# Two more buffers for gathered expert rows, placed where the streamed U tiles lie, once the last of these has been used

## The reference

```python
def gmlp_mix(xn, w_in, g_v, w_s, b_s, w_out): ...      # layer 0 token mixer
def banded_attention(q, k, v, ...): ...                # layer 1 token mixer, window of 128

def peer_ffn(xn, w_q, sub_keys, exp_u, exp_v):         # both layers, every token on its own
    ...
        q = (xb @ w_q).reshape(blk, PEER_HEADS, 2, D_HALF)
        sc = jnp.einsum('thpd,hpnd->thpn', q, sub_keys).astype(jnp.float32)
        top_s, top_i = lax.top_k(sc, PEER_TOPK)
        cand_s = top_s[:, :, 0, :, None] + top_s[:, :, 1, None, :]
        cand_i = top_i[:, :, 0, :, None] * N_KEYS + top_i[:, :, 1, None, :]
        best_s, sel = lax.top_k(cand_s.reshape(blk, PEER_HEADS, PEER_TOPK * PEER_TOPK), PEER_TOPK)
        idx = jnp.take_along_axis(cand_i.reshape(...), sel, axis=-1)
        gate = jax.nn.softmax(best_s, axis=-1)
        act = jax.nn.gelu(jnp.einsum('thkd,td->thk', exp_u[idx], xb))
        w = (gate * act.astype(jnp.float32)).astype(xb.dtype)
        return jnp.einsum('thk,thkd->td', w, exp_v[idx])

def trunk(x, ck, cv):                                  # for 512 prompt tokens and 64 sample tokens
    for l in range(DEPTH):                             # DEPTH = 2
        ...                                            # token mixer, h = h + y
        hf = rms_norm(h, norm_ffn[l]).reshape(B * L, D_MODEL)
        h = h + peer_ffn(hf, peer_w_q[l], peer_sub_keys[l], peer_u[l], peer_v[l]).reshape(B, L, D_MODEL)
        ...
```

## Time and profile before

| | |
|---|---|
| median of three runs | 3457.68 us (3442.8 to 3468.78) |
| the profiled execution | 3455.63 us, its span 3453.5 us |
| TensorE busy | 87% of the span |
| VectorE busy | 73% |
| ScalarE, GpSimd busy | 23%, 29% |
| DMA traffic | 1043.13 MB, mean 302 GB/s |
| gathers | 640 indirect DMAs, 671.13 MB |

### The profile page before, as it was taken

How to read it: one execution, slowest core, us unless ns; L and a number is a source line. 1 busy time by engine, 2 the same in 40 slices (tenths; PEclk the granted TensorE clock), 3 DMA queues, 4 the chain that set the end, 5 groups by cost and what they waited for, 6 DMA issues and landing times.

```text
span 3453.5 us, 46623 instructions
## 1 busy us (share of the span) xinstructions
PE 3012.7 (87%) x17310; PEld 2621.0 (76%) x17310; DVE 2514.5 (73%) x5433; ACT 808.9 (23%) x2386; POOL 1009.3 (29%) x840
## 2 busy tenths in 40 slices
PE   6899979999999997666688989799999999997565
PEld 6787868988888886555566857689888888885454
DVE  3377787777777778777633786988777777787777
ACT  3332212211111111111244452222111111111112
POOL 4431022222222223333254410122222222222332
PEclk9899989999999998777786978899999999998887
DMA  4225678999999999999521346679999999999996
GB/s 154 87 94 205 250 274 328 357 394 393 380 393 397 382 397 345 351 368 365 217 97 31 109 159 229 238 281 371 381 387 395 399 392 397 390 376 357 364 363 237
DMA packets 159975, 1043.13 MB, mean 302 GB/s; under 512 B 18480, under 2 KB 23920, under 8 KB 44096
## 3 DMA queue, kind: packets, MB, share of 16 engines
q0 software_dynamic: 92160, 671.13, 49.9%
q1 hardware_dynamic: 63648, 357.59, 27.5%
q10 hardware_dynamic: 4000, 12.36, 1.0%
HBM read 1033.28 MB, written 7.86 MB: 301 GB/s over the span
## 4 chain that ended last, share of the span: by engine, by line
DMA 35%; PE 32%; DVE 20%; issue 9%; ACT 1%; POOL 1%; SPq 0%; DVEq 0%; ACTq 0%; POOLq 0%
DMA gat<-uvg,idxg 35%; PE bank L695 9%; DVE acc L1568 9%; PE bank L499 7%; DVE gat L1560 3%; PE bank L486 3%; PE bank L488 3%; PE bank L487 3%; DVE oneA L1535 2%; PE bank L682 2%; DVE B L1541 2%; PE bank L584 1%; PE bank L516 1%; DVE E L1530 1%; PE bank L838 1%
## 5 line engine op out<-in xcount | busy, mean ns | idle before, releaser
L1245 POOL DMA_INDIRECT gat<-uvg,idxg x640 | 735.7, 1150 | 2074.3 <-DVE acc L1568 2005.9
L708 PE MATMUL bank<-a,V 128*128 128x256 f32 x4096 | 997.1, 406 | 216.8 <-DVE a L1552 216.6
L1560 DVE CUSTOM_DVE_ANT_0 gat<-gat,xrow 128x1024 f32<-128x1024 f32 x640 | 781.5, 1221 | 519.1 <-DMA gat<-uvg,idxg 514.8
L708 PEld LDWEIGHTS bank<-a,V 128*128 128x128 f32 x4096 | 837.3, 206 | 359.4 <-issue 230.1
L695 PE MATMUL bank<-xd,U 128*128 128x256 f32 x4096 | 926.1, 385 | 0.5 <-DMA U<-uvd 0.5
L695 PEld LDWEIGHTS bank<-xd,U 128*128 128x128 f32 x4096 | 780.4, 193 | 104.3 <-DMA U<-uvd 1.3
L1568 DVE SCALAR_TENSOR_TENSOR acc<-gat,wgt,acc 128x1024 f32<-128x1024 f32 x640 | 818.8, 1279 | 39.7 <-ACT wgt L1054 39.5
L1052 ACT ACTIVATE act<-dot 128x1 f32<-128x1 f32 x640 | 128.9, 201 | 1508.9 <-DVE dot L1560 1508.7
L682 PEld LDWEIGHTS bank<-B,oneA 128*128 128x128 f16 x4096 | 282.6, 150 | 34.0 <-DVE oneA L1535 19.4
L682 PE MATMUL bank<-B,oneA 128*128 128x32 f16 x4096 | 285.5, 246 | 19.7 <-DVE oneA L1535 17.6
L499 PE MATMUL bank<-xd,raw 128*128 128x256 f32 x1088 | 248.7, 386 | 7.5 <-DVE xd L1332 7.1
(11 more groups left out here) (192 smaller groups left out, 2278.3 us busy)
## 6 DMA issues: line engine op xcount, KB each, us to landing
U<-uvd SPq DMA_DIRECT2D x128, 1024.0 KB
V<-uvd SPq DMA_DIRECT2D x128, 1024.0 KB, 8.7
raw<-lin SPq DMA_DIRECT2D x152, 512.0 KB
gat<-uvg,idxg POOLq DMA_INDIRECT x640
hsp<-h ACTq DMA_DIRECT2D x2, 2304.0 KB, 13.9
hx<-hsp SPq DMA_DIRECT2D x2, 2304.0 KB, 13.9
sk_g<-skT ACTq DMA_DIRECT2D x2, 1024.0 KB, 4.9
sk_d<-skT ACTq DMA_DIRECT2D x2, 1024.0 KB, 8.1
```

The source lines that it names most:

```text
L708: mm = pe.matmul(bank[b][:, TD * (d % 2):TD * (d % 2) + TD], V[:, s, o:o + P], a[:, s, TD * k:TD * k + TD], start=(first and k == 0 and d ...
L1245: pool.indirect_dma_start(gat[:, s % SLOTS, :], None, uvg[l], bass.IndirectOffsetOnAxis(idxg[:, s:s + 1], 0)).then_inc(g_in[s % SLOTS], 16)
L1560: dve.tensor_tensor_reduce(gat[:, s % SLOTS, 0:D], gat[:, s % SLOTS, 0:D], xrow[:, min(s // P, 2), :], 1.0, 0.0, ALU.mult, ALU.add, dot[:, ...
```

## The change

The gathers get six buffers instead of four, for part of each layer. `slots(l)` builds a table, for every step the buffer and the step that used it last. Steps below `first` = step0(l, 40) + 2 (224 in layer 0, 226 in layer 1) use the four buffers of `gat`, steps from `first` to 311 use six (numbers 4 and 5 are `U[:, 0]` and `U[:, 1]`), and steps 312 to 319 use the four again. Each time the buffer that has rested longest is taken. Where only four are in use, the gather of step s waits for axpy(s - 4) as before; from the third of the extended steps to step 313 it waits for axpy(s - 6). The first gather into either U buffer waits for the last scores that read this buffer. The loads of "kvd" wait, beside the last scores, for the axpy of step 311. No instruction is added, removed or moved on any engine; buffers, semaphores and the values waited for change.

```diff
@@ -290,7 +290,7 @@
         a_done, sums_done, hsum_done = sem("a_done"), sem("sums_done"), sem("hsum_done")
         xr_done = sem("xr_done")
         u_in, v_in = [sem(f"u_in{s}") for s in range(2)], [sem(f"v_in{s}") for s in range(2)]
-        g_in = [sem(f"g_in{s}") for s in range(SLOTS)]
+        g_in = [sem(f"g_in{s}") for s in range(SLOTS + 2)]
         gsel_done = sem("gsel_done")
         acc_zero, dot_done, act_done, wgt_done, ax_done = (
             sem(n) for n in ("acc_zero", "dot_done", "act_done", "wgt_done", "ax_done"))
@@ -308,6 +308,29 @@
         def step0(l, i):
 
             return EARLY[l] + i * (NSTEP - EARLY[l]) // NPAIR
+
+        def slots(l):
+
+            first, last = step0(l, NPAIR - RING) + 2, NSTEP - 8
+            used, table = [-1] * (SLOTS + 2), []
+            for s in range(NSTEP):
+                k = min(range(SLOTS + 2 if first <= s < last else SLOTS), key=lambda j: (used[j], -j))
+                table.append((k, used[k]))
+                used[k] = s
+            return table
+
+        SLOT = [slots(l) for l in range(2)]
+        FILLS = [[sum(k == j for k, _ in SLOT[l]) for j in range(SLOTS + 2)] for l in range(2)]
+
+        def row(l, s):
+
+            k = SLOT[l][s][0]
+            return gat[:, k, :] if k < SLOTS else U[:, k - SLOTS, :]
+
+        def landed(l, s):
+
+            k = SLOT[l][s][0]
+            return g_in[k], 16 * (l * FILLS[0][k] + sum(j == k for j, _ in SLOT[l][:s + 1]))
 
         def scored(i):
 
@@ -371,6 +394,7 @@
             elif name == "kvd":
                 for b in range(2):
                     eng.wait_ge(full[b], BASE["peer0"][b] + NPAIR // 2)
+                eng.wait_ge(ax_done, NSTEP - 8)
             else:
                 eng.wait_ge(*tile_done(last, k))
 
@@ -1240,10 +1264,14 @@
 
             def gather(l, s):
 
-                if s >= SLOTS:
-                    pool.wait_ge(ax_done, NSTEP * l + s - SLOTS + 1)
-                pool.indirect_dma_start(gat[:, s % SLOTS, :], None, uvg[l],
-                                        bass.IndirectOffsetOnAxis(idxg[:, s:s + 1], 0)).then_inc(g_in[s % SLOTS], 16)
+                k, last = SLOT[l][s]
+                if last >= 0:
+                    pool.wait_ge(ax_done, NSTEP * l + last + 1)
+                elif k >= SLOTS:
+                    b = k - SLOTS
+                    pool.wait_ge(full[b], BASE[f"peer{l}"][b] + NPAIR // 2)
+                pool.indirect_dma_start(row(l, s), None, uvg[l],
+                                        bass.IndirectOffsetOnAxis(idxg[:, s:s + 1], 0)).then_inc(g_in[k], 16)
 
             def experts(l):
 
@@ -1556,8 +1584,9 @@
 
             def dot_x(l, s):
 
-                dve.wait_ge(g_in[s % SLOTS], 16 * (NSTEP // SLOTS * l + s // SLOTS + 1))
-                dve.tensor_tensor_reduce(gat[:, s % SLOTS, 0:D], gat[:, s % SLOTS, 0:D], xrow[:, min(s // P, 2), :],
+                u = row(l, s)[:, 0:D]
+                dve.wait_ge(*landed(l, s))
+                dve.tensor_tensor_reduce(u, u, xrow[:, min(s // P, 2), :],
                                          1.0, 0.0, ALU.mult, ALU.add, dot[:, s % 8:s % 8 + 1]).then_inc(dot_done, 1)
 
             def axpy(l, s):
@@ -1565,7 +1594,7 @@
                 n = min(s // P, 2)
                 dve.wait_ge(wgt_done, NSTEP * l + s + 1)
                 dve.wait_ge(ax_done, NSTEP * l + s)
-                dve.scalar_tensor_tensor(out=acc[:, n, :], in0=gat[:, s % SLOTS, D:RD], scalar=wgt[:, s % 8:s % 8 + 1],
+                dve.scalar_tensor_tensor(out=acc[:, n, :], in0=row(l, s)[:, D:RD], scalar=wgt[:, s % 8:s % 8 + 1],
                                          in1=acc[:, n, :], op0=ALU.mult, op1=ALU.add).then_inc(ax_done, 1)
 
             def gathered(l, s):
```

## The result

The changed kernel takes 3360.81 us (median of four runs, 3353.97 to 3364.46) against 3456.56 us before (median of four, 3442.8 to 3468.78). The ratio is 0.9725, with a 95% interval of 0.9704 to 0.9746: about 95 us less. The prediction was 3429.0 us with a range that ended at 3405, so the direction was right and the size was not: the gain is more than three times the forecast.

What follows compares the result with a forecast made beforehand. The prediction took a four-buffer ring of gather, dot and axpy to bound both layers' tails. From 3455.6 us it took 16.4 and 16.2 us, added 6 for the wait on scores: 3429.0 us, range 3405 to 3455.

Steps and rivals of the forecast that it cites:

- What bounds the kernel now: Late in each layer no engine is full; the cycle gather, dot, axpy, gather sets 3.7 us a step with four buffers.
- The tails: End of the U tiles' use to each expert stage's end: 1332 to 1687 us and 3070 to 3421 us, together 706 us.
- The pace of the ring, (L + 2.7) / 3: In the tails, a turn carries three steps; a fetch of L = 8.42 us gives 3.7 us a step, six buffers 2.2.
- L itself is mostly queueing, because the DMA engines are 93% busy: In the tails, the fetch time L, 8.42 us on the chain, was said to be mostly waiting in DMA queues.
- The speed in the tails is 358 / 0.93 = 385 GB/s ... so I keep its own speed: Tails: only the busy share rises, 0.93 to 0.975, at 385 and 383 GB/s; gains 16.4 us (layer 0), 16.2 (layer 1).
- the first rival: DMA engines also get faster per byte: both tails at 394 GB/s, 32 and 33 us gained, 3396 us; chance 0.17.
- the second rival: Memory limits the tails at 356 to 358 GB/s, pace stays 3.7 us: 3455.6 or 3462 us; chance 0.15.
- The first use of the U buffers: Switch to six buffers: free in layer 0; in layer 1 step 226's gather waits about 12 us for scores, costing 6 us.
- The third rival: Layer 1, gather of step 226: waiting on the scores costs VectorE's 10.3 us, 3466 us if nothing is gained; chance 0.08.
- The loads of "kvd": End of layer 0: four loads delayed until about 1660 us take 5.5 us and stay hidden.
- V tiles behind a deeper queue: In the tails a V tile lands in 7.9 us with some 28 us available; even doubled it stays hidden.
- VectorE "is not the limit over the tail": VectorE needs 2.8 us a step (256.6 us for 93 steps), not the limit over the tail, though near in its first part.

Runs made afterwards that it cites:

- without V: V tiles of pairs 42 to 63 cut to 16 columns: 3382.6 us from the kernel before (four buffers), 3282.61 us from the changed kernel (six).

## Why the prediction was right and wrong

**What bounds the kernel now**: right. The tails were bound by the ring gather, dot, axpy, gather, and nothing else. Taking the extra fetches away restores the old time, and the dose from three to six buffers follows.

**The pace of the ring, (L + 2.7) / 3**: right in form. It gives the pace with three buffers too: the fetch there takes 6.5 and 6.7 us on average in the two tails, (6.6 + 2.7) / 2 = 4.65, and the trace has 4.5 to 4.8 us. For the kernel before I had taken 8.42 us, the longer of the two fetches of the earlier trace rows, without a reason; that it came near the average, about 8 us by the packet records, was luck. The fetches on the chain grew, to 12.1 to 17.7 us, where 14.8 was forecast. Wrong was the sentence "L itself is mostly queueing, because the DMA engines are 93% busy": without V, at 320 GB/s, it still takes 7.3 us, and no fetch of the two tails with three buffers takes less than 5.3. The step from the old pace to the forecast did not use this sentence.

**"The speed in the tails is 358 / 0.93 = 385 GB/s ... so I keep its own speed"**: this is the step that failed, and with it both large terms of the sum. A busy share of 0.93 was read as 7% of room. The room was 15%: 358 of 421 GB/s. The share counts slow packets as busy, and there are slow packets as soon as the demand leaves pauses. So neither the share nor rate over share is a measure of what is left. Layer 0: forecast 16.4 us, measured 45.4. Layer 1, before its loss: forecast 16.2, measured 40.7 with the loss in it. The share that I forecast as 0.975 was 0.99 over the tails; the speed at full share, forecast as 385 and 383 GB/s, was 421 / 1.01 = 417 in their middle.

The row that I should have asked for was in the old trace. The DMA view of the kernel before, 1332 to 1432 us, in slices of 2.5 us, share and rate:

```profile
DMA  9999988999979997898999989999897999999997
GB/s 403 416 429 406 377 334 226 344 334 383 347 279 347 419 426 279 370 403 236 364 331 351 334 298 357 419 416 331 328 426 203 357 328 410 347 315 334 416 367 305
```

and of the changed kernel, 3100 to 3300 us, in slices of 5 us, with its traffic and queue:

```profile
GB/s 421 418 419 423 432 430 414 421 419 424 418 423 423 423 415 421 421 421 421 424 419 424 421 421 419 424 419 421 419 423 416 423 419 424 426 421 419 421 419 419
DMA packets 11380, 84.27 MB, mean 421 GB/s; under 512 B 1258, under 2 KB 1258, under 8 KB 1258
...
q0 software_dynamic: 8986, 65.41, 78.6%
```

Before, the rate swings between 203 and 429 while the share hardly moves; its peaks, 416 to 429, are what the engines can do. After, it stands at 421 all the time. With 421 GB/s in the sum the forecast would have been 127.1 MB / 421 = 302 us and 125.09 / 421 = 297 us, 53 and 54 us gained, less 6: 3355 us. The rate over the whole tails was 410 and 408, for the two ends of the stretch.

**"Then both tails run at 394 GB/s" (the first rival)**: this rival named the right thing, faster packets, and still stopped too low, at 3396 us. The stage at 2950 to 3050 us is not limited by the DMA engines. TensorE is busy for all of it, and its pace asks for two tiles and four gathers every 16 us, 6.3 MB / 16 us = 393 GB/s. I took a demand for a limit. The changed kernel runs this stage at the same 390 to 398 GB/s.

**The memory as limit (the second rival)**: refuted, also by the forecast's own row of 394, and now by 421. The Trainium skill, "DMA: Bandwidth & Descriptors", section "Specifications", has about 358 GB/s per core from HBM; here one core, the only one at work, read 421 GB/s for 200 us.

**The first use of the U buffers**: right in the main. Layer 0: GpSimd waited 3.26 us for the scores where I had forecast no wait, but VectorE did not wait. Layer 1: a wait of GpSimd of about 12 us forecast, 10.43 measured; of VectorE 10.3 forecast, 8.14 measured; 6 us of DMA time forecast, 5.6 measured. What it costs, by the tails with and without the stop, is 3 to 8 us of layer 1; the term was 6. **The third rival** had the right price for the wait and the wrong weight: the tails gave eight times as much.

**The loads of "kvd"** and **V tiles behind a deeper queue**: right that they are hidden. The loads go at 1608.53 us and are first read at 1654.65 us. VectorE's waits in the tail show no TensorE sums among them. In the run with five buffers a V tile took 9.0 us to land, against 6.8 us in the same layer before. The cost of four buffers over the last eight steps, which I had put into the share of 0.975, is 9 us in layer 0.

**VectorE "is not the limit over the tail"**: right with V (162 of 200 us busy in the middle of layer 1's tail); without V it is close to it, at 173 of 180 us, with the DMA engines full beside it.

## What to carry to other kernels

When a ring of buffers holds a transfer-bound stage, work out what the ring allows per turn and take as the next limit the peak rate that short slices of the trace reach, not the mean rate divided by the busy share. Check whether the fullest stage of the kernel is full by its limit or by its demand: bytes per turn over the time of a turn tells. Try the number of buffers as a dose; here one more buffer gave the same time as two, and the other could have gone to something else; the second was worth 5 us in layer 0, and in layer 1 it brought a stop at the switch that cost as much as it gave. Where whole times scatter by more than the effect sought, compare the stretch that the edit touches.

## What the runs showed of the hardware

The DMA engines moved 421 GB/s from HBM to one core, the only one at work, for 200 us, gathered rows of 8 KB and plain tiles mixed four to one. Their busy share says little near the top: 320 GB/s at 0.90, 358 at 0.93, 361 at 0.95, 404 at 1.00 and 421 at 1.01. A fetch of 1 MB of gathered rows took 7.3 us to land in the median while the engines had a quarter of their rate to spare (320 of 421 GB/s). Of the gathered rows' packets, which take 309 ns as a rule, 0.1% took over 400 ns while the engines were full, and 7 to 12% in three runs whose demand left pauses.
